# The gate matmuls of a gated recurrence as paired 64-row blocks, with the strips in another order

## The reference

```python
xb = xc.reshape(b, s, 12, 64)
r = sigmoid(einsum('bsgi,gij->bsgj', xb, w_r).reshape(b, s, w) + b_r)
i = sigmoid(einsum('bsgi,gij->bsgj', xb, w_i).reshape(b, s, w) + b_i)
log_a = (-8.0 * softplus(-lam)) * r
a, gated_x = exp(log_a), sqrt(-expm1(2.0 * log_a)) * (i * xc)
hs = scan(h[t] = a[t] * h[t-1] + gated_x[t])
```

## Time and profile before

| | us |
|---|---|
| time, median of 3 runs (3131.07 to 3132.6) | 3132.32 |
| the profiled execution's own time | 3131.1 |
| its span, first to last instruction | 3129.0 |
| PE busy | 3066.4 |
| DVE busy | 1791.4 |
| ACT busy | 1329.6 |
| POOL busy | 664.3 |

### The profile page before, as it was taken

One profiled execution on the slowest core, in us unless ns is written; L12 is line 12 of the kernel. 1 busy time (PEld: TensorE's weight loads), 2 busy tenths in 40 slices (PEclk: granted clock), 3 DMA queues, 4 the chain that ended last, 5 costly groups with the idle time before them and its releaser, 6 DMA issues.

```text
span 3129.0 us, 50323 instructions
## 1 busy us (share of the span) xinstructions
PE 3066.4 (98%) x18600; PEld 2608.8 (83%) x18600; DVE 1791.4 (57%) x3573; ACT 1329.6 (42%) x2637; POOL 664.3 (21%) x886
## 2 busy tenths in 40 slices
PE   7999999999999999999999999998999999999999
PEld 7988888999999888888788888888977777787777
DVE  6657674353344322345888887876353666753675
ACT  5446565454445221232333333454433555522552
POOL 3423334453542000001111111001101011032240
PEclk9999999999999999999999999999999999999999
DMA  5110011011111321122233225643100000221012
GB/s 204 37 48 18 21 35 51 28 62 44 56 59 46 103 78 51 45 95 97 72 109 109 102 101 204 196 151 140 46 28 22 16 28 15 108 72 67 28 61 101
DMA packets 77412, 231.27 MB, mean 74 GB/s; under 512 B 17712, under 2 KB 21936, under 8 KB 65648
## 3 DMA queue, kind: packets, MB, share of 16 engines
q1 hardware_dynamic: 77168, 228.05, 20.8%
HBM read 183.92 MB, written 43.84 MB: 73 GB/s over the span
## 4 chain that ended last, share of the span: by engine, by line
PE 90%; DVE 6%; ACT 2%; issue 1%; DMA 1%; SPq 0%; POOL 0%; DVEq 0%; ACTq 0%; POOLq 0%
PE ps L2546 71%; PE ps L2589 7%; PE ps L2597 3%; PE ps L2553 2%; PE ps L2604 2%; PE ps L2620 2%; PE ps L2612 1%; PE ps L2623 1%; PE ps L2640 1%; DVE wlo L2815 0%; DVE hlo L2892 0%; ACT hhi L2660 0%; ACT whi L2650 0%; DVE qk L2923 0%; DMA fa2r<-scratch_fs 0%
## 5 line engine op out<-in xcount | busy, mean ns | idle before, releaser
L2546 PE MATMUL ps<-whi,hhi 128*128 128x256 f32 (+2 forms) x1920 | 580.5, 302 | 3.0 <-DVE hlo L2892 1.7
L2546 PE MATMUL ps<-whi,hlo 128*128 128x256 f32 (+2 forms) x1920 | 563.7, 294 | 0.0
L2546 PE MATMUL ps<-wlo,hhi 128*128 128x256 f32 (+2 forms) x1920 | 563.4, 293 | 0.0
L2546 PEld LDWEIGHTS ps<-whi,hhi 128*128 128x128 f32 x1920 | 368.2, 192 | 12.8 <-issue 5.1
L2546 PEld LDWEIGHTS ps<-wlo,hhi 128*128 128x128 f32 x1920 | 368.8, 192 | 7.4 <-issue 0.2
L2546 PEld LDWEIGHTS ps<-whi,hlo 128*128 128x128 f32 x1920 | 368.2, 192 | 7.7
L2546 PE MATMUL ps<-hhi,whi 128*128 128x512 f32 x864 | 342.3, 396 | 0.0
L2546 PE MATMUL ps<-hhi,wlo 128*128 128x512 f32 x864 | 337.0, 390 | 0.0
L2546 PE MATMUL ps<-hlo,whi 128*128 128x512 f32 x864 | 336.3, 389 | 0.0
L3154 POOL TENSOR_SCALAR stats<-stats 128x2 f32<-128x2 f32 (+2 forms) x230 | 59.3, 258 | 1194.1 <-ACT xsf L2654 509.1
L3143 POOL CAST whi<-raw 128x512 fp32r<-128x512 f32 (+4 forms) x180 | 113.7, 631 | 865.8 <-PE ps L2546 856.1
(11 more groups left out here) (616 smaller groups left out, 6996.6 us busy)
## 6 DMA issues: line engine op xcount, KB each, us to landing
raw<-in_W SPq DMA_DIRECT2D x61, 1024.0 KB, 4.8
scratch_fs<-fo SPq DMA_DIRECT2D x77, 256.0 KB, 2.0
raw<-in_W SPq DMA_DIRECT2D x24, 768.0 KB, 4.3
wd<-in_WD SPq DMA_DIRECT2D x44, 256.0 KB, 3.5
wf0b<-in_WF SPq DMA_DIRECT2D x10, 1024.0 KB, 5.3
wf1b<-in_WF SPq DMA_DIRECT2D x10, 1024.0 KB, 5.2
scratch_x<-x SPq DMA_DIRECT2D x16, 512.0 KB, 3.3
orw<-scratch_outs SPq DMA_DIRECT2D x6, 1024.0 KB, 5.8
```

Source lines behind the costliest of these rows:

```text
L2546: x = e.matmul(r.out, a, b, start=(r.start and m == 0), stop=(r.stop and m == n - 1), skip_group_check=r.joined)
```

## The change

`lw` becomes one 128x128 matrix per strip: rows 0 to 63 hold block 0's matrices for r and i side by side, rows 64 to 127 block 1's for i and r. Each half of the tokens is one item with two matmuls, one of the upper 64 rows and one of the lower, into two banks. In the first bank partitions 0 to 63 are r and 64 to 127 are i of block 0; in the second 0 to 63 are i and 64 to 127 are r of block 1. ACT does four tanh of 64x512 for a half, each into its place in `rg` or `ig`; the i bias is turned by 64 rows to lie on the partitions that it is read at. The item of a half stands right behind the gate half's attention step, with one step behind it, so a strip has 6 steps, and strip 2 has 8.

```diff
-        lw = rest("lw", [6, 2, 128], F, 64 * KB + 512)
+        lw = rest("lw", [6, 128], F, 64 * KB + 512)
@@ strip loop, for hf in range(2), behind the gate half and its step
-            ch.done(m)
-            if s == 5:
-                h_free = [m]
-                y_split(0, (0, 1), y_made)
-                w_pump(ws["split"])
-            for gi, (dst, bias) in enumerate(((rg, ex), (ig, zq))):
-                for hf in range(2):
-                    r = Rec()
-                    r.cut = slice(hf * 512, hf * 512 + 512)
-                    r.place, r.w, r.conv, r.free = DB.take(), lw[:, s, gi, :], L.conv[hf], prev
-                    r.dst, r.bias = dst[:, r.cut], bias[:, s:s + 1]
-                    emit("lru_gate", r)
-                    L.gates = r.place.read
-                    m = r.place.full
+                if hf:
+                    ch.done(m)
+                    if s == 5:
+                        h_free = [m]
+                        y_split(0, (0, 1), y_made)
+                        w_pump(ws["split"])
+                r = Rec()
+                r.s, r.cut = s, slice(hf * 512, hf * 512 + 512)
+                r.places, r.conv, r.free = [DB.take(), DB.take()], L.conv[hf], prev
+                emit("lru_gate", r)
+                L.gates = r.places[1].read
                 next(att_steps, None)
-            next(att_steps, None)
+            for _ in range(2 if s == 2 else 0):
+                next(att_steps, None)
@@ tensor
-                    w.wait_ge(*r.place.before)
+                    for place in r.places:
+                        w.wait_ge(*place.before)
                     w.wait_ge(*r.conv)
                     w.wait_ge(*t_lw)
-                    e.matmul(r.place.ps[:, :], r.w, xc[:, r.cut], start=True, stop=True).then_inc(r.place.full[0], 1)
+                    for place, rows in zip(r.places, (slice(0, 64), slice(64, 128))):
+                        x = e.matmul(place.ps[:, :], lw[rows, r.s, :], xc[rows, r.cut], start=True, stop=True)
+                        x.then_inc(place.full[0], 1)
@@ scalar
+                    for place, parts in zip(r.places, (((rg, ex, up_, up_), (ig, zq, down_, up_)),
+                                                       ((ig, zq, up_, down_), (rg, ex, down_, down_)))):
+                        w.wait_ge(*place.full)
+                        for x, (dst, bias, src, to) in enumerate(parts):
+                            w.wait_ge(*w.last)
+                            a = e.activation(dst[to, r.cut], place.ps[src, :], ACT.Tanh, scale=0.5, bias=bias[src, r.s:r.s + 1])
+                            a.then_inc(w.sig(place.read) if x else w.inner(), 1)
```

More of the change, by code:

```diff
@@ L2388, in build @@
                                       for i, n in enumerate(("xc", "rg", "ig", "av", "tv", "hs", "gg"))]
-        lw = rest("lw", [6, 2, 128], F, 64 * KB + 512)
-        t_lw = load("lruw", lw[:, :, :, :], d["lruw"], free1, ln_tok[7])
+        lw = rest("lw", [6, 128], F, 64 * KB + 512)
+        t_lw = load("lruw", lw[:, :, :], d["lruw"], free1, ln_tok[7])
         t_kv1b = load("kv1b", kv[0][:, :, :, :], d["kv1"], t_kv1, o2_last)
@@ L2789, in _ @@
                 elif kind == "lru_gate":
-                    w.wait_ge(*w.last)
-                    w.wait_ge(*r.place.full)
                     w.wait_each(r.free)
                     w.wait_ge(*t_lm)
-                    e.activation(r.dst, r.place.ps[:, :], ACT.Tanh, scale=0.5, bias=r.bias).then_inc(w.sig(r.place.read), 1)
+                    up_, down_ = slice(0, 64), slice(64, 128)
+                    for place, parts in zip(r.places, (((rg, ex, up_, up_), (ig, zq, down_, up_)),
[5 more added lines that the diff above has]
+                            a.then_inc(w.sig(place.read) if x else w.inner(), 1)
                 elif kind == "decay_exp":
@@ L3222 @@
         "conv_w": a["lru_conv_w_2"][0].reshape(4, 6, 128).transpose(2, 1, 0).reshape(128, 24),
-        "conv_b": feat(a["lru_conv_b_2"]), "b_r": feat(a["lru_b_rgate_2"]), "b_i": feat(a["lru_b_igate_2"]),
+        "conv_b": feat(a["lru_conv_b_2"]), "b_r": feat(a["lru_b_rgate_2"]), "b_i": np.roll(feat(a["lru_b_igate_2"]), 64, axis=0),
         "lru_lam": feat(a["lru_lambda_2"]),
@@ L3226 @@
     }
-    lruw = np.zeros((128, 6, 2, 128), np.float32)
-    for gi, name in enumerate(("lru_w_rgate_2", "lru_w_igate_2")):
-        for blk in range(12):
-            o = 64 * (blk % 2)
-            lruw[o:o + 64, blk // 2, gi, o:o + 64] = a[name][0, blk]
+    both = [a[name][0].reshape(6, 2, 64, 64) for name in ("lru_w_rgate_2", "lru_w_igate_2")]
+    lruw = np.stack([np.concatenate([both[x][:, x], both[1 - x][:, x]], axis=2) for x in range(2)], axis=1)
+    lruw = lruw.reshape(6, 128, 128).transpose(1, 0, 2)
     tab_a, tab_b, tab_m = tables()
```

## The result

The changed kernel takes 3156.19 us (median of 4 runs, 3155.59 to 3157.17) against 3131.78 in the same set of runs: ratio 1.0079, 95% interval 1.0067 to 1.0092. It is slower by 24.4 us. The forecast, 3147, had the direction, but the measured time lies above its 3141 to 3152.

The account below looks back on a forecast made before the run. Before, PE bounds the kernel; after, a closed ACT/DVE loop does. Loops sum to 171.3 us, putting the last dense half 14.6 later: 3131.1 + 14.6 = 3145.7, plus 1.2 for the median, 3147. Range 3141 to 3152, lowered to 3138 for partly closed loops.

Parts of the forecast that it names:

- the closed loop: From one second gate half through ACT and DVE to the next: 34.6 us a strip against PE's 30.4.
- The pair on PE: Two 64-row gate matmuls overlap: 1.06 us plus about 0.1 to enter, 1.16 instead of 1.72.
- The half-height tanh at 0.72: ACT's gate tanh of 64x512: half the rows save nothing, 24 x 0.72 = 17 us more on ACT.
- the last wait: PE before the second gate half, until DVE's gate product frees its bank; ends 1.4 us after the value product's input copy.
- the gate half's bank: Bank the second gate half takes from the first, freed only by DVE's gate product (L3077); a wait for PE.
- the value product's input: DVE's copy (L2968) needed by the odd step behind pair 0; a second wait, followed by that step's 1.07 us.
- PE idles about 4.2 per strip: In the recurrence's strips: loop of 34.6 us against PE's own work of 30.4.
- The tail: From the last dense half to the end: nothing changes, about 99 us as before.
- The start: Strip 0's second gate half begins at 2867.8 instead of 2866.39, behind pair 0, two transposes and an entry.
- PE as the bound: Rival: PE stays the recurrence's bound, 4.4 us less before the last dense half, 3128 us; chance 0.07.

Follow-up runs that it names:

- the two full tanh: Two 128x512 tanh a half instead of four 64x512: against the changed kernel 3145.93 us (new order), against the form alone 3128.07 us (old order).
- PE kept at work: Changed kernel, with pair 0 issued three times more ahead of the one that counts in strips 1 to 4; 3149.07 us.
- order alone: Changed kernel's new order, but with the 128-row matmuls and two full tanh a half of before; 3141.83 us.
- the form alone: Against the kernel before: paired 64-row matmuls and four half-height tanh a half, in the order of before; 3143.05 us.
- the kernel with pair 0 early: The form alone, but in strip 5 pair 0 stands behind the first gate half; 3141.07 us.

## Why the prediction was wrong

The direction and the closed loop were right. One term was missing: what a wait of PE costs beyond its length. I go through the forecast in its own steps.

- **The pair on PE, 1.06 and 0.1 to enter.** Right. Pair 0 of strip 0 stands in the chain with the length taken from the earlier trace rows:

```profile
2867.90 1.06 PE ps L2640 x4
2868.96 0.37 PE ps L2595 x2
2869.33 5.49 PE ps L2544 x24
```

The second gate half starts 1.43 us behind the pair's start; 1.36 was forecast.
- **The half-height tanh at 0.72.** Right: 48 at 0.683 us, where the 128x512 ones of before take 0.687, and ACT has 16.3 us more (17 forecast). That it lies on the loop is shown by the two full tanh (in the new order five loops of 174.1 us, 2868.02 to 3042.09, in place of 181.2; in the old 15 us in all, of which a share is the clock's).
- **The closed loop, 34.6 us against PE's 30.4.** Right in kind and size where the clock stays up: 34.8 to 35.1 with PE kept at work, 33.4 without the two tanh more, where 33.2 follows. PE idles 20.3 us in five strips, 4.1 a strip, where 4.2 was forecast. The 0.2 to 0.5 over come mostly from the last wait: I had the gate half's bank last and the value product's input 0.3 before it. The profile has a third one last, the value product's bank, which DVE frees 0.65 us behind that input (L3088, L3090 in the chain above). Then the odd step's 1.07 still comes: in all about 0.4 more than the way over the gate half's bank. The forecast does not name this bank, and the wait that it named in front of the second gate half does not show up.
- **What a wait of PE costs.** This is the term that failed. I priced the idle time at its length, and all of PE's work behind it at the durations of before, all taken at the full clock. The sum "PE idles about 4.2 per strip" stood there, and I didn't ask what it does to the clock. By the chain, second gate half of strip 0 to that of strip 5: forecast 171.3 us, measured 3050.54 - 2869.33 = 181.2; with PE kept at work 172.7 (2868.20 to 3040.86). So 8.5 of the 9.9 us missing in the loops are the clock, 1.4 the bank and the rest of the loop's error. The pieces add up to about the same: the dense halves (7.04 + 7.11 + 6.66 + 7.02) less four times 5.49 is 5.9 us, and the four odd steps took 7.4 us where they take 4.6 with PE kept at work. The Trainium skill, "TensorE: Matmul & The Clock Gate", section "HAM oscillation — how this bites in real kernels", describes such a case: there waits for DMA between groups of matmuls let the gate throttle PE, so that each group starts cold. The windows of strip 1 agree, with 0.50 behind the wait; those of strip 5, with 1.00 behind one of 2.99 us, do not.
- **The tail.** Right: the last dense half ends at 3050.54 + 5.57 = 3056.1, and the span 99.1 us later, as before. PE's last long piece starts 25.9 us behind the start of that dense half, against 25.8 before:

```profile
3050.54 5.57 PE ps L2544 x24
...
3076.44 71.25 PE ps L2544 x312
```

- **The start.** 1.5 us of the profile's 26.2 stand ahead of the change, since pair 0 begins at 2867.90 where the same place of before is 2866.39. In the other kernels of this order the place is at 2866.6 to 2868.5, so that is how executions differ. The medians differ by 24.4.
- **The rivals.** PE as the bound is refuted for the change. But its price of 4.4 us is nearly what the form gives with ACT relieved (2.9). The order of before was not on my list of things that the form might spoil: I believed it would gain 2.7 there, and it lost 12.6. The same thing I had worked out for the new order holds in the old one: before's own sequence on ACT and DVE is nearly as long as PE's work. The kernel with the two full tanh shows it, where PE does wait for banks: its strips are 31.3, 32.3, 31.5 and 29.6 us against before's 31.3, 33.9, 31.4 and 29.8. By these differences before had between nothing and 1.6 us of slack a strip, an estimate from two kernels. It was hidden behind a PE at 100% with ACT at 48% of the stretch (81.10 of 168.00).

What stays open: how the 2.9 us of the form with two tanh divide into the 5.6 us that PE saves and the waits for two banks at once; what of the new order's 11.4 us (order alone) is the odd step's place and what the turn of the banks, since I moved neither by itself; and why the same wait lowered the clock in strips 1 to 4 and not in strip 5.

## What to carry to other kernels

A stage in which one engine is busy all the time can still be within a few per cent of a loop through the others: before adding work to a half-idle engine, follow the sequence from its result to the next thing that the full engine needs, and compare its length with that engine's. ACT's time here went by the elements along a partition (0.683 us for 64x512, 0.687 for 128x512), so a form that halves the rows of each result and doubles their number doubles ACT's work, whatever PE saves. And an idle stretch of PE of some us can cost more than its length, since the matmuls behind it may run at half clock: here about 2 us a time (8.5 us over 4 gaps), and nothing in a fifth gap of the same length. So a range should have both.

## What the runs showed of the hardware

Two 64-row fp32 matmuls of 512 columns into two banks take 1.06 us together, two 128-row ones 1.72. At the lower clock the pair takes about twice as long, 1.96 us as the record of four passes in the form alone, against 1.13. No length of wait decided the clock in these runs. Waits of 2.95 us in the changed kernel were followed by 0.50 in four strips, one of 2.99 us by 1.00. Waits of 2.92 us in front of pair 1 were followed by the slow pair in strip 1 of the form alone and by one of full speed (1.13) in strip 3 of the kernel with pair 0 early. One of 1.71 us in the order alone left the clock at 1.00, and behind one of 1.75 us in strip 4 of the form alone the pair took 2.08. A filler of useless matmuls in the gap, 24 of them, made the kernel 7.1 us faster.
